# Eight modulation chunks summed over channels on VectorE instead of multiplied on TensorE, in a two-layer hybrid transformer step

## What is computed

```python
for l in range(DEPTH):
    m_ctx = jnp.split(jax.nn.silu(c_ctx) @ mod_w[l] + mod_b[l], 6, axis=-1)
    m_lat = jnp.split((jax.nn.silu(c) @ mod_w[l] + mod_b[l])[:, None, :], 6, axis=-1)
    hp = _modulate(xp, m_ctx[0], m_ctx[1])      # x * (1 + scale) + shift
    hs = _modulate(xs, m_lat[0], m_lat[1])
    # layer 0: yp, ys = recurrent part (HGRN2) and latent attention (8 heads), projected out
    # layer 1: yp, ys = gated convolutions
    xp = _layer_norm(ALPHA * xp + m_ctx[2] * yp, ln_g[l, 0], ln_b[l, 0])
    # mixture of experts on _modulate(xp, m_ctx[3], m_ctx[4]), gated by m_ctx[5]; the same for xs
```

## Time and profile before

| | |
|---|---|
| median of three runs | 1292.52 us |
| lowest and highest | 1288.12 and 1296.45 us |
| the profiled execution's own time | 1289.75 us |
| its span, first to last instruction | 1287.9 us |
| mean granted TensorE clock in it | 0.978 of full speed |
| busy in the span: TensorE matmul, VectorE, ScalarE, GpSimd | 92%, 46%, 27%, 15% |

### The profile page before, as it was taken

One profiled execution on the slowest core, in us unless ns is written; L12 is line 12 of the kernel. 1 busy time (PEld: TensorE's weight loads), 2 busy tenths in 40 slices (PEclk: granted clock), 3 DMA queues, 4 the chain that ended last, 5 costly groups with the idle time before them and its releaser, 6 DMA issues.

```text
span 1287.9 us, 17510 instructions
## 1 busy us (share of the span) xinstructions
PE 1188.9 (92%) x6755; PEld 680.1 (53%) x6755; DVE 597.9 (46%) x1173; ACT 352.0 (27%) x695; POOL 186.9 (15%) x177
## 2 busy tenths in 40 slices
PE   5999999999999989999999877999999998999774
PEld 2554555545546577456555435755555555555441
DVE  2223333310136666768432217079986865332218
ACT  1333444421214543212122125311023111221122
POOL 1000000010000001131323120800000332222210
PEclk9999999999999999998999898999999998999988
DMA  9504476773211204826799969021114438999973
GB/s 348 210 25 177 142 254 239 289 270 114 89 33 40 74 10 163 340 83 232 299 407 409 406 244 393 23 91 66 66 66 171 156 128 316 392 410 408 354 293 150
DMA packets 99666, 269.79 MB, mean 209 GB/s; under 512 B 12811, under 2 KB 15154, under 8 KB 98690
## 3 DMA queue, kind: packets, MB, share of 16 engines
q1 hardware_dynamic: 83632, 234.55, 48.3%
q0 software_dynamic: 15632, 34.02, 7.1%
q10 hardware_dynamic: 322, 0.12, 0.0%
HBM read 257.68 MB, written 31.93 MB: 225 GB/s over the span
## 4 chain that ended last, share of the span: by engine, by line
PE 78%; DVE 6%; DMA 6%; SPq 4%; ACT 3%; issue 2%; ACTq 0%; POOLq 0%; DVEq 0%
PE ps L2285 18%; PE ps L2296 14%; PE ps L2797 8%; PE ps L2814 4%; PE ps L2175 4%; PE ps L2437 3%; DMA ln_rows<-in_moe_w_up 3%; PE ps L2600 3%; PE ps L2785 2%; PE ps L2581 2%; PE ps L2404 2%; PE ps L2746 2%; SPq L710 1%; PE ps L2699 1%; SPq L707 1%
## 5 line engine op out<-in xcount | busy, mean ns | idle before, releaser
L2285 PE MATMUL ps<-h_cm,weights 128*128 128x512 f32 (+1 forms) x832 | 226.8, 434 | 0.0
L2285 PEld LDWEIGHTS ps<-h_cm,weights 128*128 128x128 f32 x832 | 126.3, 191 | 104.0 <-issue 103.7
L2296 PE MATMUL ps<-weights,mix_cm 128*128 128x512 f32 x256 | 112.2, 595 | 0.0
L1769 DVE SCALAR_TENSOR_TENSOR scratch<-scratch,taps_cm 128x655 f32<-128x655 f32 x120 | 101.5, 897 | 2.5 <-ACT scratch L1325 1.0
L2296 PEld LDWEIGHTS ps<-weights,mix_cm 128*128 128x128 f32 x256 | 47.9, 190 | 56.5 <-issue 56.4
L2067 DVE TENSOR_TENSOR scratch<-ps,scratch 128x128 f32<-128x128 f32 x38 | 11.1, 292 | 143.1 <-ACT scratch L1373 143.1
L2296 PE MATMUL ps<-weights,h_cm 128*128 128x512 f32 (+1 forms) x208 | 71.4, 502 | 0.0
L2797 PE MATMUL ps<-weights,scratch 128*64 128x256 f32 x384 | 68.3, 389 | 1.8 <-DMA weights<-in_moe_w_up 1.8
L1442 DVE COPY mod_parts<-ps 128x512 f32<-128x512 f32 x24 | 16.6, 691 | 93.3 <-PE ps L2175 93.3
L1697 DVE SCALAR_TENSOR_TENSOR mix_cm<-mix_cm,gate_rows,ps 128x128 f32<-128x128 f32 x152 | 46.0, 345 | 25.1 <-PE ps L2545 23.0
L2296 PEld LDWEIGHTS ps<-weights,h_cm 128*128 128x128 f32 x208 | 36.3, 190 | 35.6 <-issue 35.6
(11 more groups left out here) (449 smaller groups left out, 2133.1 us busy)
## 6 DMA issues: line engine op xcount, KB each, us to landing
weights<-in_mod_w SPq DMA_DIRECT2D x13, 2048.0 KB, 8.9
x_tm<-in_mod_w SPq DMA_DIRECT2D x10, 2048.0 KB, 8.6
weights<-in_moe_w_gate SPq DMA_DIRECT2D x24, 512.0 KB, 11.6
weights<-in_moe_w_up SPq DMA_DIRECT2D x24, 512.0 KB, 13.4
weights<-in_moe_w_down SPq DMA_DIRECT2D x24, 512.0 KB, 15.7
scratch<-in_moe_w_down SPq DMA_DIRECT2D x21, 512.0 KB, 12.9
weights<-in_ab_w_in SPq DMA_DIRECT2D x5, 2048.0 KB, 12.8
weights<-in_cd_w_in SPq DMA_DIRECT2D x5, 2048.0 KB, 16.0
```

What stands on the lines that cost most here:

```text
L1769: ins = V.scalar_tensor_tensor(out=CO[:, j, 0:655], in0=UP[:, j, k:k + 655], scalar=CW[:, 4 * k + j:4 * k + j + 1], in1=CO[:, j, 0:655], o ...
L2285: ins = T.matmul(ps(*name)[:, a:b], w[:, k, col:col + 128], HT[:, k, a:b], start=(k == 0), stop=(k == KD - 1))
L2296: ins = T.matmul(ps(*name)[:, at:at + w.shape[2]], src[:, k, t * 128:t * 128 + 128], w[:, k, :], start=(k == 0), stop=(k == KD - 1))
```

## The change

Layer 1's chunks 4 to 11 (`VEC_MODS`) no longer go through `mod_product`. `vec_mod(c)` sums a chunk's eight blocks of 128 channels on VectorE, for each of the two vectors: two TENSOR_SCALAR and 14 SCALAR_TENSOR_TENSOR of 128 partitions x 512 columns, each waiting for the one before, into `VEC_PARTS[c % 2]`. What is left, a sum over 128 partitions, is `vec_mod_sum(c)` on TensorE: four matmuls with ones (128 x 32) and 256 moving columns, into the four 32-column groups. `vec_mod_row(c)` copies 256 columns to `MR`, and SP's `store_vec_row` writes them with two DMAs.

Chunk 4's first eight instructions stand in VectorE's steps 18 and 19 of the attention (four each), the other eight right behind it, then chunk 5, and from there on each chunk is followed by the row copy of the one before. The sums stand on TensorE behind five of the first six projections (after `hq` (0,1), (0,2), (0,3), (1,0), (1,1)), then behind (1,3), `hv` 0 and `hv` 2. `value_rows(0)`, which stood behind `mod_sums(1)`, comes behind chunk 11, the last row copy between `value_rows(2)` and `value_rows(3)`; `mod_sums(1)` is now two instructions and stands in step 2 of the recurrent stage. In the attention, the products are left in steps 1, 2, 4, 5, 7, 9, 10, 12, 14, 15 and 17; steps 6, 11, 16 and 19 have none. `mod_sums(0)` moves from step 18 to step 15, and the loads of the query weights move ahead by three chunks. A sixth weight slot, in `scratch` behind the last scores, makes three slots (1, 4, 5) for the chunks. The core of the diff:

```diff
@@ -113,11 +113,14 @@
 
-ATTN_MODS = [(0, c) for c in range(4, 12)] + [(1, c) for c in range(8)]
-MOD_STEP = {5 * p + t: 4 * p + i for p in range(4) for i, t in enumerate((0, 1, 2, 4)) if p or t}
+ATTN_MODS = [(0, c) for c in range(4, 12)] + [(1, c) for c in range(4)]
+MOD_STEP = {n: i + 1 for i, n in enumerate((1, 2, 4, 5, 7, 9, 10, 12, 14, 15, 17))}
 KEY_STEP = {0: 1, 6: 2, 11: 3}
 QUERY_STEP = {3: 1, 8: 2, 13: 3}
-PROJ_MODS = {(0, 0): (1, 8), (0, 1): (1, 9), (0, 3): (1, 10), (1, 2): (1, 11)}
+VEC_MODS = list(range(4, 12))
+VEC_SUM_AT = {("hq", 0, 1): 4, ("hq", 0, 2): 5, ("hq", 0, 3): 6, ("hq", 1, 0): 7, ("hq", 1, 1): 8, ("hq", 1, 3): 9,
+              ("hv", 0): 10, ("hv", 2): 11}
+VEC_STEPS = {18: range(0, 4), 19: range(4, 8)}
 
@@ -534,22 +540,26 @@
-            return W[:, 4096 * s:4096 * (s + 1)] if s < 3 else (OTF[:, 0:4096] if s == 3 else XF[:, 0:4096])
+            if s < 3:
+                return W[:, 4096 * s:4096 * (s + 1)]
+            return (OTF[:, 0:4096], XF[:, 0:4096], Z[:, 10240:14336])[s - 3]
...
-        in_slot = [None, None, None, None, ("rows",)]
+        in_slot = [None, None, None, None, ("rows",), ("keys",)]
...
+        WITEM["keys",] = {"last": ("s", 7, 4)}
...
-            words_in[s] += 16 * len(parts)
-            WITEM[name] = {"slot": s, "full": s, "value": words_in[s], "parts": parts, "last": last, "before": in_slot[s]}
+            full = s if s < 5 else 3
+            words_in[full] += 16 * len(parts)
+            WITEM[name] = {"slot": s, "full": full, "value": words_in[full], "parts": parts, "last": last, "before": in_slot[s]}
@@ -581,28 +591,28 @@
             mod_item(l, c, 4 if a % 2 else 1)
-            if a == 11:
+            if a == 8:
                 hq_item(1, 2)
-            if a == 13:
+            if a == 10:
                 hq_item(0, 0)
-        mod_item(1, 8, 1)
-        mod_item(1, 9, 4)
-        mod_item(1, 10, 1)
-        proj_item(("hv",), 1, ("hv", 4), w_in, 1536, 2048)
-        mod_item(1, 11, 4)
+        for c, s in zip(VEC_MODS, (1, 4, 5, 1, 4, 5, 4, 5)):
+            if c == 10:
+                proj_item(("hv",), 1, ("hv", 4), w_in, 1536, 2048)
+            mod_item(1, c, s)
         proj_item(("hfb",), 0, ("fb", 3), w_in, 1024, 1536)
...
         N_ITEMS0 = len(items)
-        in_slot[:] = [None, None, None, None, None]
+        in_slot[:] = [None] * 6
         for n, c in enumerate(CD_ORDER):
...
         MOD_DMAS = 16 * 10
-        ROW_MODS = [m for m in ATTN_MODS + [(1, c) for c in range(8, 12)] if m[1] >= 4]
+        ROW_MODS = [m for m in ATTN_MODS if m[1] >= 4]
+        VEC_PARTS = [z(14336, 1024).rearrange("p (g n) -> p g n", g=2), OTF[:, 0:1024].rearrange("p (g n) -> p g n", g=2)]
 
@@ -649,7 +659,10 @@
-                filled(sp, *WITEM[name]["last"])
+                if name[0] == "mod" and name[1] == 1 and name[2] in VEC_MODS:
+                    sp.wait_ge(mod_summed, 2 + VEC_MODS.index(name[2]))
+                else:
+                    filled(sp, *WITEM[name]["last"])
@@ -658,12 +671,22 @@
+            def store_vec_row(c):
+
+                emptied(sp, "modv", c)
+                for g in range(2):
+                    sp.dma_start(PARTD[1, 0, c // 2 - 2, g, 512 * (c % 2):512 * (c % 2) + 512].rearrange("(h n) -> h n", h=2),
+                                 MR[64 * g:64 * g + 64:32, c % 2, 0:256]).then_inc(d_mr[c % 2], 16)
+
...
-                    sp.wait_ge(d_mr[i], 64 * (4 * l + 4))
+                    sp.wait_ge(d_mr[i], 256 + 128 * l)
...
-                sp.dma_start(MOD_PARTS[l], PARTD[l].rearrange("j i g (k c) -> (i g k) j c", k=8)).then_inc(d_mod, 16)
+                if l == 0:
+                    sp.dma_start(MOD_PARTS[l], PARTD[l].rearrange("j i g (k c) -> (i g k) j c", k=8)).then_inc(d_mod, 16)
+                else:
+                    sp.dma_start(MOD_PARTS[l][:, 0, :], PARTD[l, 0].rearrange("i g (k c) -> (i g k) c", k=8)).then_inc(d_mod, 16)
@@ -671,7 +694,7 @@
-                sp.wait_ge(mod_summed, l + 1)
+                sp.wait_ge(mod_summed, 1 + l * (len(VEC_MODS) + 1))
@@ -717,12 +740,15 @@
                     load_item(n)
-                    if items[n] == ("mod",) + ATTN_MODS[14]:
+                    if items[n] == ("mod",) + ATTN_MODS[10]:
                         load_parts(0)
-                    if items[n] == ("mod",) + ATTN_MODS[15]:
+                    if items[n] == ("mod", 1, 4):
                         store_mods(0)
+                    if items[n][0:2] == ("mod", 1) and items[n][2] >= 8:
+                        store_vec_row(items[n][2] - 4)
                     if items[n] == ("hfb",):
-                        store_row(1, 11)
+                        for c in range(8, 12):
+                            store_vec_row(c)
                         load_parts(1)
@@ -1441,11 +1467,42 @@
+            def vec_mod(c, steps_of_it=range(16)):
+
+                it = WITEM["mod", 1, c]
+                acc = VEC_PARTS[c % 2]
+                w = slot3(it["slot"])[:, 0:4096].rearrange("p (k n) -> p k n", k=8)
+                for i in steps_of_it:
+                    k, g = i // 2, i % 2
+                    if i == 0:
+                        dve.wait_ge(w_full[it["full"]], it["value"])
+                    if k == 0:
+                        chain(V.tensor_scalar(acc[:, g, :], w[:, 0, :], CT[:, 0, g:g + 1], None, ALU.mult))
+                    else:
+                        ins = V.scalar_tensor_tensor(out=acc[:, g, :], in0=w[:, k, :], scalar=CT[:, k, g:g + 1], in1=acc[:, g, :],
+                                                     op0=ALU.mult, op1=ALU.add)
+                        if i < 15:
+                            chain(ins)
+                        else:
+                            ins.then_inc(mod_summed, 1)
+
+            def vec_mod_row(c):
+
+                filled(dve, "modv", c)
+                if c < 6:
+                    filled(dve, "modb", 1, c - 2)
+                else:
+                    dve.wait_ge(d_mr[c % 2], 256 + 32 * ((c - 4) // 2))
+                release(V.tensor_copy(MR[:, c % 2, 0:256], ps("modv", c)[:, 0:256]), "modv", c)
+
...
+                if l:
+                    V.tensor_scalar(MOD_SUM[32:48, :], MOD_SUM[32:48, :], 1.0, None, ALU.add).then_inc(mod_summed, 1)
+                    return
@@ -1579,9 +1636,14 @@
                     mod_row(*ATTN_MODS[MOD_STEP[n - 1]])
-                if n == 18:
+                if n == 15:
                     mod_sums(0)
-            mod_row(*ATTN_MODS[15])
+                if n in VEC_STEPS:
+                    vec_mod(VEC_MODS[0], VEC_STEPS[n])
+            vec_mod(VEC_MODS[0], range(8, 16))
+            for c in VEC_MODS[1:]:
+                vec_mod(c)
+                vec_mod_row(c - 1)
 
@@ -1661,20 +1723,18 @@
 
-            for c in range(2):
-                for j in range(4):
-                    if (c, j) in PROJ_MODS:
-                        mod_row(*PROJ_MODS[c, j])
+            value_rows(0)
             dve.wait_ge(h_zero, 5)
...
             decay_arguments(0)
-            mod_sums(1)
-            value_rows(0)
+            value_rows(1)
             emptied(dve, "hq", 0, 3)
...
             carried_rows(0)
-            for t in range(1, NT):
-                value_rows(t)
+            value_rows(2)
+            vec_mod_row(VEC_MODS[-1])
+            value_rows(3)
+            value_rows(4)
             for i in range(20):
@@ -1704,6 +1764,8 @@
                 dve.wait_ge(h_state, i + 1)
+                if i == 2:
+                    mod_sums(1)
                 if i >= 11:
@@ -2185,6 +2247,17 @@
+            def vec_mod_sum(c):
+
+                pe.wait_ge(mod_summed, 2 + VEC_MODS.index(c))
+                open_group(pe, "modv", c)
+                for g in range(2):
+                    for h in range(2):
+                        at = 32 * (2 * g + h)
+                        ins = T.matmul(ps("modv", c)[at:at + 32, 0:256], const("ones")[:, 0:32],
+                                       VEC_PARTS[c % 2][:, g, 256 * h:256 * h + 256], start=True, stop=True)
+                close_group(ins, "modv", c)
+
@@ -2504,11 +2577,13 @@
                         close_group(weighted_values(19, ps("o", 3, 4)[:, 0:128]), "o", 3, 4)
-                    if (c, j) in PROJ_MODS:
-                        mod_product(*PROJ_MODS[c, j])
+                    if ("hq", c, j) in VEC_SUM_AT:
+                        vec_mod_sum(VEC_SUM_AT["hq", c, j])
             w = w8(weights(pe, "hv"))
...
                 project_tm(("hv", t), HT, t, [(0, w)])
+                if ("hv", t) in VEC_SUM_AT:
+                    vec_mod_sum(VEC_SUM_AT["hv", t])
             for t in range(NT):
```

More of the change, by code:

```diff
@@ L204, in psum_groups @@
                         g.append(("o", 3, 4))
-                    if (c, j) in PROJ_MODS:
-                        g.append(("mod",) + PROJ_MODS[c, j])
-            g += [("hv", t) for t in range(NT)]
+                    if ("hq", c, j) in VEC_SUM_AT:
+                        g.append(("modv", VEC_SUM_AT["hq", c, j]))
```

(4 more changed lines are left out.)

## The result

The changed kernel took 1279.46 us, median of five runs (1277.82 to 1280.42), against 1292.52 before: the ratio is 0.9895, 95% interval 0.9877 to 0.9913, so 1.05% faster (0.9 to 1.2%). The forecast was 1280. The profiled execution took 1279.76 us with a span of 1278.0, 9.9 less than before.

A forecast was written before the change was run, and what follows sets the result against it. TensorE was taken as the bound (78% of the chain), with VectorE largely free in the projections. Attention 9.0 + projections 2.4 = 11.4 us off: profiled 1289.75 becomes 1278.3, from the median 1281.1; named 1280, range 1274 to 1289.

The forecast's parts named there:

- The attention, 9.0 us off: Attention: four modulation products leave and turns move, 3.7 + 2.6 + 0.9 + 1.75 = 9.0 us off, bounds 6.5 to 9.5.
- Steps 17 to 19: End of the attention: first projection starts at 267.87 instead of 269.62, 1.75 us off, with step 19's product in it.
- The limits that I named: Attention: step 17's 1.04 us weight wait goes, step 19's maximum starts at 263.56, nothing is late behind a removed product.
- The projections, 2.4 us off: Recurrent part's projections: 105.0 + 4.0 + 1.0 = 110.0 us against 112.4, bounds 3.9 off to 3 us on.
- 8 x 0.5: Projections: eight added `vec_mod_sum` on TensorE at 0.50 us each, 4.0 us.
- The wait at chunk 8: Projections: only chunk 8's sum comes late from VectorE; TensorE stands still 1.0 us, between 0 and 3.
- 105.0: Projections: us for eight query and forget projections, the attention's last output and five value projections, without the modulation products.
- The rival of a bound VectorE: Projections: chunks come late, TensorE waits at nearly every sum; 1301.5 us at 1.0 us an instruction; chance 0.06.
- its break-even: Projections: the whole gain is taken back at a VectorE period of 14.1 us, or 0.88 us an instruction.
- The recurrent stage and all behind it: Recurrent stage: `mod_sums(1)` in step 2 and the later gate-weight load cost nothing; each step as before.
- two starting points 2.8 us apart: Whole kernel: profiled execution 1289.75 becomes 1278.3; from the median of three runs, 1292.52, it would be 1281.1.
- The 1.5 us per chunk: VectorE: by the skill's semaphore rule a chunk would be some 1.5 us shorter, the wait would vanish, 1 us less.

## Why the prediction was right

**The attention, 9.0 us off: right.** The steps ahead of step 17's product were to give 7.24 us. The two first profiles have the same early fall of the clock (32 to 37 us) and can be compared directly: the scores of step 17 start at 246.06 instead of 253.30, which is 7.24. Steps 17 to 19 were to give 1.75 with the DMA wait in it. From those scores to the first projection it was 16.32 us; it is 5.04 to the product and 9.53 from there with the clock up, 1.75 less. Four products put back cost 8.3 us: 7.3 of their own and 1.6 by the clock, less a wait of 0.56 at chunk 8 that went. The limits that I named held too: the DMA wait is gone, the maximum of step 19 starts 5.21 us behind the product where the forecast's times give 5.15 (258.41 to 263.56), and nothing was late behind the removed products.

**What it missed there** is what those last 1.5 us of waiting do. I had counted them much as before (0.51 and 0.72 us then, 0.88 and 0.66 now), with TensorE's clock left out of the count. In five of the six profiles that have them a lower clock followed, which cost 1.3 to 2.8 us.

**The projections, 2.4 us off: half right.** With the clock up the stretch to the recurrent stage went from 113.48 to 112.23, 1.25 us. The term "8 x 0.5" measured 8 x 0.57 = 4.6. The wait at chunk 8 was to be 1.0 and was 0.56, at the place named and nowhere else. The term "105.0" for the untouched work was too small. A projection takes 8.66 us from start to start between two of its kind, 8.75 with one of its kind on one side and 8.85 with none; each place where the row is broken costs 0.18 us, for the value blocks too. The row is broken in nine places where it was in four, so the same work took 106.0. These three, 0.6 and 1.0 us too little and 0.4 too much, are terms of the sum that were mis-sized; the mechanism stands.

**VectorE:** period 12.27 us for 12.25, 752 ns for 747, chunk 8 the critical one, and room behind chunk 11: the last value copy waits 4.4 us for TensorE. The row copy of chunk 4 ties the rest: it waits for TensorE's sum, so VectorE's later chunks are counted from that sum on, and a slow first projection doesn't make TensorE wait at chunk 8 (the first profile), while a fast one does.

**The rival of a bound VectorE** did not come true, but its break-even was nearly met: at a period of 13.8 us the time was 1291.4, within noise of before, where 14.1 was given. Partly that is luck: 3 us of it are the clock, which the rival did not have. Without them the gain would not have been wholly gone.

**The recurrent stage and all behind it: nothing, within what can be seen.** From its first matmul to the end of the span it is 904.8 and 907.1 us in the two profiles of the kernel before, and 902.9, 904.5 and 910.3 in the three of the changed kernel, the last with a mean granted clock of 0.96 there instead of 0.97. The stretches of the change account for 10.2 us (9.0 and 1.25). The medians differ by 13.1 in the first set and by 10.9 and 12.2 in the later ones, which the spread of single runs (up to 10 us within a set) leaves open.

**The number itself** is partly luck. With 10.2 us off instead of 11.4 the profiled execution would have been at 1279.5. It was at 1279.76, but with 2.2 us lost by the clock's fall up to the recurrent stage and 1.9 us less behind that stage's start, neither of which was forecast. And 1280 was chosen between two starting points 2.8 us apart.

14 chained instructions of 752 ns take 10.99 us, which leaves (10.99 - 14 x 0.752) / 13 = 0.035 us between them, as the rows of before had shown. The Trainium skill (VectorE: DVE Perf Modes, The DRAIN you can't avoid) says that a semaphore behind each operation adds nothing to what the pipeline's emptying costs anyway; the section also says that an instruction which isn't held starts earlier. The trace agrees with the second: the chained ones leave a gap, while the unchained copy of 0.69 us at 253.10 overlaps the instruction that starts at 253.70. The 1.5 us per chunk that I had drawn from the first did not come: a chunk takes 12.0 us (294.86 to 306.88). No run takes the semaphores away, so what they add by themselves is not shown.

## What to carry to other kernels

Work moved from a full engine to a free one is worth what the full engine's instructions take, if one counts, for each hand-over, when the other will be done: here one number, VectorE's period per chunk, decided, and 13% more of it gave all back, a third of that by way of the clock. At the border of two stages, keep the moved work out of the short chain that the full engine waits for, even where it seems to fit: 1.5 us of waiting there were followed in most profiles by one to three more of clock, and without that work in the chain the stages were 1.25 us shorter even with the clock up. And compare stages, not whole times, when the clock falls at other places in each execution.

## What the runs showed that was not expected

- At the attention's end, two waits of 0.88 and 0.66 us (once 1.73 and 0.72) were followed by 4 to 8 us at the lower clock in six of seven profiles; in the six with at most 1.23 us of waiting in the same steps, none was. A single wait of 2.52 us and one of 4.36 were followed by 4 and 7 us at the lower clock. A wait of 2.52 us at chunk 7 was not, nor were the 2.27 and 2.52 us in three pieces of the kernel before.
- A projection takes 8.66 us between two of its kind and 8.85 between other matmuls: a group of small matmuls set into the row costs 0.18 us beside its own 0.57.
- VectorE's three-operand instruction kept its 752 ns beside full matmuls and beside loads at 371 GB/s.
